# Forward substitution in the top half of a triangular solve, and level tiles of 64 columns, in the scan of an RWKV-7 layer on one NeuronCore

## The chip, the cores and the metric

The kernel runs on one core of a Trainium2 chip. The metric is the device time of one execution in microseconds (us); the time before is 1505.27 us, the median of three runs. Engines: TensorE (PE for its products, PEld for the loads of weights, which run beside the products), VectorE (DVE), ScalarE (ACT), GpSimd (POOL), SyncE (SP, which issues most transfers).

## What is computed

A decoder trunk of two blocks over 256 tokens of 1024 channels in float32: a pooling and gating mixer with a dense feed-forward block, then an RWKV-7 time mixing with 16 heads of 64 channels and a block of experts (two of eight per token). The change lies in the time mixing. Its core is a recurrence over the tokens with a 64 x 64 state per head:

```python
def step(S, inp):
    r_t, w_t, k_t, v_t, kk_t, a_t = inp
    sa = jnp.einsum('bhij,bhj->bhi', S, -kk_t)
    S = (S * w_t[:, :, None, :]
         + sa[..., None] * (kk_t * a_t)[:, :, None, :]
         + v_t[..., None] * k_t[:, :, None, :])
    y = jnp.einsum('bhij,bhj->bhi', S, r_t)
    return S, y
_, ys = lax.scan(step, S0, (tmajor(rh), tmajor(wh), tmajor(kh), tmajor(vh), tmajor(kk), tmajor(ah)))
```

## The kernel before

The kernel is written for each engine by hand: each engine's instructions stand in the order of its function, and semaphores tie the engines together. The time mixing takes its 256 tokens in two chunks (`c` = 0, 1) of 128. Within a chunk the recurrence is a triangular system per head: with a strictly lower triangular A (128 x 128), the kernel needs U = (I - A)^-1 R. R, the right side, is the product of a second causal matrix with the values and, in chunk 1, a product with the state `ST`. From U come the outputs and, in chunk 0, the state.

**The inverse.** `XT[c]` holds the transposed inverse, built bottom up. VectorE inverts the diagonal blocks of 16 tokens for all heads together, column by column (`recur`, 15 steps of two instructions, fed by TensorE's `block_rows`). `spread` puts them on the diagonal of `XT`. Then come the levels `v` = 0, 1, 2, which join blocks of 16 to 32, of 32 to 64 and of 64 to 128. A level is: `turned` (TensorE transposes `XT` by the identity, ScalarE copies its even blocks to `Xv`), `level_Y` (A times those), a masked copy to `Yv` on VectorE, `level_X` (Y times the odd blocks), and an add into the odd blocks of `XT` on VectorE. The third level is written as `top_Y` and `top_X`, with copies on ScalarE. After it `solved` multiplies the whole inverse (128 x 128) with the right side, and VectorE copies the result to `Us`.

**The order on TensorE.** The heads are handled in two groups of eight (`pair`). Levels of chunk 0 alternate with `block_rows(1, ...)`, which feed VectorE's `recur(1, ...)`. Levels of chunk 1 alternate with the group norm of chunk 0 (`gn_mean`, `head_sums`, `head_spread`). 22 transposes of the identity without use stand ahead of the first `turned(0, 0)`. There ScalarE also clears the two `Yv` tiles (semaphore `level_Y_zeroed`). On VectorE, `masked(0, gg)` makes parts of A causal, which the right side and the outputs need (semaphore `scan_A_causal`). After `outputs(1)` come the group norm, the output projection (`wo`), the router and the experts. The experts' weights come through SyncE's queue into the `ring` buffer; their first four loads wait for places in the scan (`level_X`, `U`, `Y`).

In the profile's shapes, 128*64 is a weight tile of 128 rows and 64 columns, and 64*64 one of 64 rows and 64 columns. A float32 product of the kernel stands there as two instructions with a load of weights each; a transpose stands as one.

Of the kernel before, what the change touches and what calls it, by code (L numbers as in the profile page):

```python
# [43 lines left out]
for _name, _w in (("ident", 128), ("ones", 128), ("upto", 128), ("before", 128), ("upto2", 128), ("heads", 128), ("iota", 128),  # L44
                  ("cum", 256), ("blk16", 128), ("mask4", 64), ("mask5", 64), ("eye16", 16), ("par", 2), ("hsel", 142),
                  ("invcnt", 4 * T)):
    CONST[_name] = (CW, CW + _w)
    CW += _w
# [7 lines left out]
def constants():  # L56
# [15 lines left out]
    put("blk16", s // 16 == t // 16)  # L72
    h4, h5 = np.arange(64)[None, :] // 16, np.arange(64)[None, :] // 32
    put("mask4", (s // 32 == h4) & (s % 32 >= 16))
    put("mask5", (s // 64 == h5) & (s % 64 >= 32))
# [31 lines left out]
def trunk(nc, I, cst_dram, cols_dram, out, stop=None):  # L107
    ctx = ExitStack()
    with ctx:
# [285 lines left out]
        def rows_product(pe, lhs, w, bank, done):  # L395
# [21 lines left out]
        l_tr, l_xe, l_y, l_yd, l_ya, l_xu, l_xd, l_x6 = (sem(x) for x in (  # L417
            "level_T", "level_T_copied", "level_Y", "level_Y_masked", "top_Y_copied", "level_X", "level_X_added",
            "top_X_copied"))
# [51 lines left out]
        XT = [ru(4 + c).rearrange("p (g l t) -> p g l t", g=4, l=4) for c in range(2)]  # L471
        Yv = [ru(6 + v).rearrange("p (g l t) -> p g l t", g=4, l=4) for v in range(2)]
        Xv = [wu(3, 1024, 1024 * v).rearrange("p (g l t) -> p g l t", g=4, l=4) for v in range(2)]
        Y6 = ru(13, 1024).rearrange("p (g n) -> p g n", g=4)
# [3 lines left out]
        Us = flatT[:, 0:1024].rearrange("p (g n) -> p g n", g=4)  # L478
# [35 lines left out]
        def lev(c, v, pair):  # L514

            return 6 * c + 2 * v + pair + 1

        def masked_at(c, v, pair):

            return 4 * c + 2 * v + pair + 1  # L520

        def turned_at(c, v, n):

            return 12 * c + 4 * v + n + 1

        TURN_BANK = (0, 1, 4, 5)
# [60 lines left out]
        def rwkv_pe(pe):  # L587
# [157 lines left out]
            def right_side(c, pair):  # L745
                pe.wait_ge(a_pm, 4 * c + 2 * pair + 2)
                pe.wait_ge(l_xe, turned_at(c, 2, pair))
                for gg, l, k, o, at in heads_of(pair):
                    dst = psum[:, pair, at:at + HD]
                    last = nc.tensor.matmul(dst, A_all[c][:, gg, l, 2, :], v_row[:, c * D + k * P + o:c * D + k * P + o + HD],  # L750
                                            start=True, stop=(c == 0))
                    if c == 1:
                        last = nc.tensor.matmul(dst, AR[:, k, c, 0, :], ST[:, k, o:o + HD], start=False, stop=True)
                last.then_inc(t_r, 1)

# [3 lines left out]
            pe.wait_ge(y_zero, 3)  # L759

            def turned(c, v):
                for gg in range(4):
                    if v == 0:
                        pe.wait_ge(x_full, 2 * c + gg // 2 + 1)
                        if c == 1 and gg == 2:
                            pe.wait_ge(t_sc, 2)
                    elif v == 2 and gg >= 2:
                        pe.wait_ge(l_xd, masked_at(c, 1, 1))
                    else:
                        pe.wait_ge(l_xd, masked_at(c, v - 1, gg // 2))  # L770
                    for l in range(4):
                        last = nc.tensor.transpose(psum[:, TURN_BANK[gg], l * P:(l + 1) * P], XT[c][:, gg, l, :], ident)
                    last.then_inc(l_tr, 1)

            def level_Y(c, v):
                for pair in range(2):
                    pe.wait_ge(l_xe, turned_at(c, v, 2 * pair + 1))
                    if v == 0 and c == 1:
                        pe.wait_ge(t_yc, pair + 1)
                    for gg, l, k, o, at in heads_of(pair):  # L780
                        for i in range(2):
                            hs, n = slice(HD * i, HD * i + HD), slice(32 * i, 32 * i + 32)
                            last = nc.tensor.matmul(psum[hs, 2 + pair, at + 32 * i:at + 32 * i + 32], A_all[c][hs, gg, l, 0, hs],
                                                    Xv[v][hs, gg, l, n], start=True, stop=True)
                    last.then_inc(l_y, 1)

            def level_X(c, v, pair):
                pe.wait_ge(l_yd, masked_at(c, v, pair))
                if pair == 0:
                    pe.wait_ge(l_xe, turned_at(c, v, 3))  # L790
                for gg, l, k, o, at in heads_of(pair):
                    odd = XT[c][:, gg, l, :].rearrange("p (b h t) -> p b h t", h=2, t=B0 << v)[:, :, 1, :]
                    for i in range(2):
                        hs, n = slice(HD * i, HD * i + HD), 2 >> v
                        last = nc.tensor.matmul(psum[hs, 4 + pair, at + 32 * i:at + 32 * i + 32], Yv[v][hs, gg, l, hs],
                                                odd[hs, n:2 * n, :] if i else odd[hs, 0:n, :], start=True, stop=True)
                last.then_inc(l_xu, 1)

            def top_Y(c):
                for pair in range(2):  # L800
                    pe.wait_ge(l_xe, turned_at(c, 2, 2 * pair + 1))
                    for gg, l, k, o, at in heads_of(pair):
                        last = nc.tensor.matmul(psum[HD:P, 2 + pair, at:at + HD], A_all[c][:, gg, l, 0, HD:P],
                                                Xv[0][:, gg, l, :], start=True, stop=True)
# [1668 lines left out]
```

## Time and profile before

| | |
|---|---|
| median of three runs | 1505.27 us (1505.21 to 1505.7) |
| the profiled execution | 1507.26 us, span 1505.4 us |
| granted TensorE clock, mean | 0.996 of full speed |
| busy share: PE, DVE, ACT, POOL | 98%, 83%, 67%, 1% |
| first turn of chunk 0's levels on TensorE | at 414.46 us |
| outputs of chunk 0, of chunk 1 on TensorE | at 445.16 us, at 486.66 us |
| first product of the experts | at 542.01 us |

The span is the time from the first to the last instruction of the profiled execution, which took 1.86 us more than it and 1.99 us more than the median of the runs. The scan's levels and their ends fill some 75 us of the 1505; the experts, from 542 us on, fill most of the rest. Times in the timeline view count from the span's start. A view can show an instruction up to 0.1 us earlier or later than the chain of work does, where instructions overlap.

### The profile page before, as it was taken

To read this page: it belongs to the slowest core of one execution; us is meant where nothing else is said; L and a number is where in the kernel's file an instruction comes from. 1 tells how busy PE (TensorE), PEld (TensorE's weight loads), DVE (VectorE), ACT (ScalarE), POOL (GpSimd) and SP (SyncE) were. 2 spreads that over 40 slices of the span, in tenths; PEclk is the share of its full clock that TensorE was granted. 3 is DMA by queue.
4 is the path that set the end of the run, shared out by engine and by line. 5 is a ranking of instruction groups with operands and counts; after the bars stand their busy time and mean duration, and the time that the engine had idled before them with its cause. 6 is when DMAs were issued, how large, how long until landed. Compare 5 with 4: busy or idle time off the path is not lost.

```text
span 1505.4 us, 22041 instructions
## 1 busy us (share of the span) xinstructions
PE 1474.2 (98%) x8088; PEld 1226.9 (82%) x8088; DVE 1242.6 (83%) x1375; ACT 1009.8 (67%) x1157; POOL 22.2 (1%) x19
## 2 busy tenths in 40 slices
PE   8999999999899999999999999999999999999997
PEld 5888888799798588888888888888888888888885
DVE  3756666787885289999999999999999999999997
ACT  2544444663523178888888888888888878888885
POOL 0000000000000020000000000000000000000200
PEclk9999999999999999999999999999999999999998
DMA  9889553036405499999999999999999999999990
GB/s 361 326 271 301 175 168 112 1 117 217 141 2 178 174 322 372 395 392 395 396 392 396 394 368 388 390 365 383 394 366 373 393 386 362 395 380 362 349 369 28
DMA packets 206696, 453.57 MB, mean 301 GB/s; under 512 B 8881, under 2 KB 46257, under 8 KB 206386
## 3 DMA queue, kind: packets, MB, share of 16 engines
q1 hardware_dynamic: 203154, 446.12, 80.6%
q0 software_dynamic: 1280, 4.20, 1.1%
q10 hardware_dynamic: 2208, 2.50, 0.5%
q8 instruction: 38, 0.62, 0.2%
q14 instruction: 16, 0.13, 0.0%
HBM read 437.58 MB, written 23.60 MB: 306 GB/s over the span
## 4 chain that ended last, share of the span: by engine, by line
PE 92%; DVE 5%; ACT 2%; DMA 1%; issue 0%; DVEq 0%; ACTq 0%
PE psum L1591 20%; PE psum L1593 20%; PE psum L1592 20%; PE psum L2401 5%; PE psum L2404 3%; PE psum L902 2%; PE psum L2325 2%; PE psum L2365 2%; PE psum L2366 2%; PE psum L2367 2%; PE psum L600 2%; PE psum L1609 2%; PE psum L2318 1%; PE psum L696 1%; DVE time_mix_parts L1150 1%; PE psum L722 1%
## 5 line engine op out<-in xcount | busy, mean ns | idle before, releaser
L1799 DVE TENSOR_TENSOR w_lo<-ring,w_hi 128x1024 fp32r<-128x1024 f32 x672 | 811.0, 1224 | 63.5 <-ACT w_hi L1693 15.8
L1693 ACT ACTIVATE w_hi<-ring 128x1024 fp32r<-128x1024 f32 x672 | 711.3, 1062 | 172.5 <-PE psum L1593 172.4
L1591 PE MATMUL psum<-w_hi,xg_split 128*128 128x512 f32 x896 | 353.5, 395 | 0.3 <-DVE xg_split L1890 0.3
L1593 PE MATMUL psum<-w_lo,xg_split 128*128 128x512 f32 x896 | 349.4, 390 | 0.0
L1592 PE MATMUL psum<-w_hi,xg_split 128*128 128x512 f32 x896 | 348.8, 389 | 0.0
L1593 PEld LDWEIGHTS psum<-w_lo,xg_split 128*128 128x128 f32 x896 | 168.1, 188 | 35.8
L1591 PEld LDWEIGHTS psum<-w_hi,xg_split 128*128 128x128 f32 x896 | 168.3, 188 | 34.1 <-DVE xg_split L1890 0.6
L1592 PEld LDWEIGHTS psum<-w_hi,xg_split 128*128 128x128 f32 x896 | 168.4, 188 | 33.6
L1591 PE MATMUL psum<-w_hi,ht_split 128*128 128x512 f32 x448 | 176.0, 393 | 0.0
L1593 PE MATMUL psum<-w_lo,ht_split 128*128 128x512 f32 x448 | 174.6, 390 | 0.0
L1592 PE MATMUL psum<-w_hi,ht_split 128*128 128x512 f32 x448 | 174.4, 389 | 0.0
L2235 DVE TENSOR_TENSOR f_lo<-ring,f_hi 128x1024 fp32r<-128x1024 f32 x66 | 79.5, 1223 | 51.3 <-ACT f_hi L2124 51.3
L2124 ACT ACTIVATE f_hi<-ring 128x1024 fp32r<-128x1024 f32 x66 | 69.0, 1056 | 52.4 <-PE psum L2404 30.6
L1591 PEld LDWEIGHTS psum<-w_hi,ht_split 128*128 128x128 f32 x448 | 84.1, 188 | 19.4 <-issue 2.3
L1593 PEld LDWEIGHTS psum<-w_lo,ht_split 128*128 128x128 f32 x448 | 84.1, 188 | 17.8
L1592 PEld LDWEIGHTS psum<-w_hi,ht_split 128*128 128x128 f32 x448 | 84.1, 188 | 17.1
L2401 PE MATMUL psum<-x_split,f_hi 128*128 128x512 f32 x352 | 88.9, 393 | 0.9 <-DVE x_split L360 0.4
L2401 PEld LDWEIGHTS psum<-x_split,f_hi 128*128 128x128 f32 x352 | 63.6, 189 | 14.2 <-DVE x_split L360 1.4
L600 PE MATMUL psum<-mixed_parts,time_mix_parts 128*128 128x256 f32 x448 | 64.6, 283 | 1.4 <-DVE time_mix_parts L1150 1.0
L600 PEld LDWEIGHTS psum<-mixed_parts,time_mix_parts 128*128 128x128 f32 x448 | 58.4, 192 | 1.7 <-DVE time_mix_parts L1150 1.2
L2404 PEld LDWEIGHTS psum<-x_split,f_lo 128*128 128x128 f32 x352 | 48.0, 190 | 3.4
L2404 PE MATMUL psum<-x_split,f_lo 128*128 128x256 f32 x352 | 49.1, 282 | 0.0
(370 smaller groups left out, 1488.7 us busy)
## 6 DMA issues: line engine op xcount, KB each, us to landing
ring<-o_moe_wg_dram SPq DMA_DIRECT2D x56, 2048.0 KB, 10.8
ring<-o_moe_wu_dram SPq DMA_DIRECT2D x56, 2048.0 KB, 11.3
ring<-o_moe_wd_dram SPq DMA_DIRECT2D x56, 2048.0 KB, 11.3
ring<-e_ffn_wg_dram SPq DMA_DIRECT2D x11, 1024.0 KB, 5.5
ring<-e_ffn_wu_dram SPq DMA_DIRECT2D x11, 1024.0 KB, 8.7
ring<-e_ffn_wd_dram SPq DMA_DIRECT2D x11, 1024.0 KB, 11.1
expert_rows<-work SPq DMA_DIRECT2D x1, 8192.0 KB, 27.9
ring<-e_w_in_dram SPq DMA_DIRECT2D x2, 2048.0 KB, 18.1
```

The costliest lines, as they stand in the source:

```text
L600: last = nc.tensor.matmul(psum[0:rows, n % 8, 0:width], l, r, start=(i == 0), stop=(i == len(lhs_rhs) - 1))
L902: return nc.tensor.matmul(psum[:, n, :], YT[:, k, (n // 2) * P:(n // 2 + 1) * P], wo_s[n % 2][:, k, :], start=(k == 0), stop=(k == KT - 1))
L1591: nc.tensor.matmul(dst, x_hi, hi, start=first, stop=False)
L1592: nc.tensor.matmul(dst, x_lo, hi, start=False, stop=False)
L1593: return nc.tensor.matmul(dst, x_hi, lo, start=False, stop=last_)
L1609: last = nc.tensor.transpose(psum[:, 6, f * P:(f + 1) * P], SIL[c % 2][:, f * P:(f + 1) * P], ident)
L1693: nc.scalar.activation(w_hi[:, (4 * i + n) % 4, :], piece(i, n), ACT.Copy).then_inc(m_hi, 1)
L1799: V.tensor_tensor(w_lo[:, r, :], piece(i, n), w_hi[:, r, :].bitcast(F32), ALU.subtract).then_inc(m_lo, 1)
L2124: nc.scalar.activation(as_piece(f_hi, i, what), ffn_piece(what, c, n), ACT.Copy).then_inc(f_phi, 1)
L2235: nc.vector.tensor_tensor(as_piece(f_lo, i, what), ffn_piece(what, c, n), as_piece(f_hi, i, what).bitcast(F32), ALU.subtract).then_inc(f_p ...
L2401: nc.tensor.matmul(psum[:, bank, :], hi[:, k, :], x_tile(k).rearrange("p h t -> p (h t)"), start=(k == 0), stop=False)
L2404: last = nc.tensor.matmul(psum[:, bank, T:2 * T], lo[:, k, :], x_tile(k)[:, 1, :], start=False, stop=(k == KT - 1))
```

## The change

The third level goes. In its place the system is solved in two halves of 64 tokens. `right_side` makes the top half of R, `solved` multiplies it with the top half's inverse (64 x 64), and the result `Us` is copied by ScalarE. Then `right_side` makes the low half, with one product more per head that subtracts A's lower left quarter times the top of `Us`, and `solved` multiplies it with the low half's inverse. `XT`, `Xv` and `Yv` keep only the diagonal quarters, so each tile is 64 columns wide. `turned` no longer transposes 128 x 128 tiles. It multiplies each 64 x 64 quarter with the even columns of the identity, so that only those blocks are made. The add in `level_X` becomes one instruction over 128 rows, the two clears and `spread` cover half the columns, and the four `masked(0, gg)` each move one place ahead on VectorE. GpSimd's clear of `Y6` goes.

```diff
             def turned(c, v):
-                for gg in range(4):
+                for pair in range(2):
...
-                    for l in range(4):
-                        last = nc.tensor.transpose(psum[:, TURN_BANK[gg], l * P:(l + 1) * P], XT[c][:, gg, l, :], ident)
+                    for gg, l, k, o, at in heads_of(pair):
+                        for hs in tops:
+                            even = ident[:, hs].rearrange("p (b h t) -> p b h t", h=2, t=B0 << v)[hs, :, 0, :]
+                            last = nc.tensor.matmul(psum[hs, pair, at // 2:at // 2 + 32], XT[c][hs, gg, l, :], even,
+                                                    start=True, stop=True)
                     last.then_inc(l_tr, 1)
...
+            top, low = slice(0, HD), slice(HD, P)
+
+            def solved(c, pair, rows):
+                if rows == top:
+                    pe.wait_ge(l_xd, lev(c, 1, pair))
+                    pe.wait_ge(t_rc, 4 * c + pair + 1)
+                else:
+                    pe.wait_ge(t_rc, 4 * c + 2 + pair + 1)
+                for gg, l, k, o, at in heads_of(pair):
+                    last = nc.tensor.matmul(psum[rows, 4 + pair, at:at + HD], XT[c][rows, gg, l, :],
+                                            Rs[rows, gg, HD * l:HD * l + HD], start=True, stop=True)
+                last.then_inc(t_u, 1)
+
+            def right_side(c, pair, rows):
+                pe.wait_ge(a_pm, 4 * c + 2 * pair + 2)
+                if rows == low:
+                    pe.wait_ge(t_uc, 4 * c + pair + 1)
+                upto = slice(0, rows.stop)
+                for gg, l, k, o, at in heads_of(pair):
+                    dst = psum[rows, pair, at:at + HD]
+                    vv = v_row[upto, c * D + k * P + o:c * D + k * P + o + HD]
+                    last = nc.tensor.matmul(dst, A_all[c][upto, gg, l, 2, rows], vv, start=True, stop=(c == 0 and rows == top))
+                    if c == 1:
+                        last = nc.tensor.matmul(dst, AR[:, k, c, 0, rows], ST[:, k, o:o + HD], start=False, stop=(rows == top))
+                    if rows == low:
+                        last = nc.tensor.matmul(dst, A_all[c][top, gg, l, 0, low], Us[top, gg, HD * l:HD * l + HD],
+                                                start=False, stop=True)
+                last.then_inc(t_r, 1)
...
-            turned(1, 2)
-            right_side(1, 0)
-            top_Y(1)
-            right_side(1, 1)
-            top_X(1)
-            solved(1)
+            for rows in (top, low):
+                for pair in range(2):
+                    right_side(1, pair, rows)
+                for pair in range(2):
+                    solved(1, pair, rows)
             outputs(1)
```

On TensorE, behind the second level of chunk 0 and its block products, the kernel before has the third turn (L772), the right side (L750), top Y (L803) and the next block products (L722). The shape in a row is that of the output.

```order
L772 MATMUL psum<-cst,ring 128x128 [waits level_X_added]
L772 MATMUL psum<-cst,ring 128x128 x3
L750 MATMUL psum<-work,ring 128x64 [waits level_T_copied,scan_A_causal]
L750 MATMUL psum<-work,ring 128x64 x7
L803 MATMUL psum<-work,ring 64x64 [waits level_T_copied,level_Y_zeroed]
L803 MATMUL psum<-work,ring 64x64 x7
L803 MATMUL psum<-work,ring 64x64 [waits level_T_copied]
L803 MATMUL psum<-work,ring 64x64 x7
L722 MATMUL psum<-work,xnT 128x64 [waits column_product]
```

At the same place the changed kernel has the right side's top half (its L799) around the block products (L713), and solved (L787) for both groups of heads.

```order
L799 MATMUL psum<-work,ring 64x64 [waits scan_A_causal]
L799 MATMUL psum<-work,ring 64x64 x7
L713 MATMUL psum<-work,xnT 128x128 [waits column_product]
L713 MATMUL psum<-work,xnT 128x112
L713 MATMUL psum<-work,xnT 128x96
L713 MATMUL psum<-work,xnT 128x80
L799 MATMUL psum<-work,ring 64x64 [waits scan_A_causal]
L799 MATMUL psum<-work,ring 64x64 x7
L787 MATMUL psum<-ring 64x64 [waits R_copied,level_X_added]
L787 MATMUL psum<-ring 64x64 x7
```

The turn of 128 x 128 tiles is gone, and solved comes ahead of the last block products, over 64 rows and columns.

Further on in chunk 1, the changed kernel's TensorE has this in the low half of the right side: the second matrix times the values (L799, weights of 128 rows), the state's product (L801, 128 rows) and A's quarter times the top of U (L803, 64 rows), head after head.

```order
L799 MATMUL psum<-work,ring 64x64 [waits U_copied,scan_A_causal]
L801 MATMUL psum<-work 64x64
L803 MATMUL psum<-ring 64x64
L799 MATMUL psum<-work,ring 64x64
L801 MATMUL psum<-work 64x64
L803 MATMUL psum<-ring 64x64
L799 MATMUL psum<-work,ring 64x64
L801 MATMUL psum<-work 64x64
```

Before, the right side of chunk 1 was one row of products whose weights were all 128 rows by 128 columns. Now weights of 128 and of 64 rows follow one another within each head.

## Rows read from the trace of the kernel before

**Rows 1.** The page: busy time of each engine, share of the span, instructions.

```profile
PE 1474.2 (98%) x8088; PEld 1226.9 (82%) x8088; DVE 1242.6 (83%) x1375; ACT 1009.8 (67%) x1157; POOL 22.2 (1%) x19
```

**Rows 2.** Waits after 530 us: who for whom, us in total, times, longest.

```profile
ACT w_hi L1693 <- PE psum L1593: 172.4, 572, 2.5
```

**Rows 3.** Stretches: busy time (instructions) by engine, PE clock, DMA share, GB/s.

```profile
400.00:500.00 100.00, 95.14 (x1282) 83.68 (x1281) 64.32 (x144) 34.63 (x63) 0.94 (x1) 1.00 0.31 109
...
532.00:533.00 1.00, 1.00 (x6) 1.00 (x5) 0.93 (x6) 1.00 (x2) 0.00 (x0) 0.50 1.05 430
...
640.00:740.00 100.00, 100.00 (x457) 82.72 (x456) 93.05 (x86) 81.98 (x88) 0.00 (x0) 1.00 1.04 394
```

**Rows 4.** Timeline from 410 us: start, length, instruction, [idle before <- what ended it].

```profile
410.70 3.71 ACT L1094 ACTIVATE ring<-cst 128x2048 f32<-128x2048 f32 x2
410.86 2.38 PEld L758 LDWEIGHTS psum<-cst 128*128 128x128 f32 x22 [1.52 <-ACT ring L1044]
...
414.46 1.97 PE L772 MATMUL psum<-cst,ring 128*128 128x128 f32 x16 [0.98 <-ACT ring L1094]
```

**Rows 5.** Timeline, turns of the levels that waited, chunk 0 and 1.

```profile
423.88 1.09 PE L772 MATMUL psum<-cst,ring 128*128 128x128 f32 x8 [0.64 <-DVE ring L1319]
...
454.40 1.06 PE L772 MATMUL psum<-cst,ring 128*128 128x128 f32 x8 [0.44 <-DVE work L1380]
...
461.91 1.98 PE L772 MATMUL psum<-cst,ring 128*128 128x128 f32 x16 [0.83 <-DVE ring L1319]
```

**Rows 6.** Chain of work, chunk 0: start, us to the next piece, what.

```profile
416.43 1.99 PE psum L783 x64
...
431.01 1.93 PE psum L772 x16
...
434.67 2.01 PE psum L803 x32
...
441.51 3.71 PE psum L822 x32
445.23 0.38 PE psum L835 x4
```

**Rows 7.** Timeline of TensorE: third turn, outputs of chunk 1, experts' first product.

```profile
469.50 2.26 PE L772 MATMUL psum<-cst,ring 128*128 128x128 f32 x16
...
486.66 0.19 PEld L834 LDWEIGHTS psum<-work 128*64 128x64 f32 x2
...
542.01 0.50 PE L1591 MATMUL psum<-w_hi,xg_split 128*128 128x512 f32 x1 [0.32 <-DVE xg_split L1890]
```

**Rows 8.** Timeline, loads of weights of L803 and of what follows.

```profile
434.60 1.94 PEld L803 LDWEIGHTS psum<-work,ring 128*64 128x64 f32 x32
...
436.61 0.97 PEld L722 LDWEIGHTS psum<-work,xnT 128*128 128x128 f32 x8
```

**Rows 9.** Timeline where the weights' shape changes without a semaphore.

```profile
446.74 0.44 PE L836 MATMUL psum<-ring,work 128*64 128x128 f32 x4
...
447.10 0.30 PEld L842 LDWEIGHTS psum<-xnT,xn 128*128 128x128 f32 x2 [0.17 <-issue]
...
297.08 3.72 PE L633 MATMUL psum<-ring,work 128*128 128x256 f32 x16
...
300.73 0.74 PEld L636 LDWEIGHTS psum<-ring,work 32*128 32x128 f32 x16 [0.33 <-issue]
```

**Rows 10.** Stretches of 0.01 us, L803 alone: products (in flight), loads, clock, DMA.

```profile
434.70:434.71 0.01, 0.01 (x1) 0.01 (x2) 1.00 0.00 0
434.71:434.72 0.01, 0.01 (x2) 0.01 (x3) 1.00 0.00 0
```

**Rows 11.** Groups from 410.8 to 494 us: busy us, mean ns, idle before.

```profile
L803 PE MATMUL psum<-work,ring 128*64 128x64 f32 x64 | 4.2, 224 | 0.0
...
L1061 ACT ACTIVATE ring<-psum 64x512 f32<-64x512 f32 x4 | 2.4, 592 | 1.6 <-PE psum L803 1.6
...
L1319 DVE TENSOR_TENSOR ring<-ring,psum 64x256 f32<-64x256 f32 x16 | 6.6, 416 | 0.3
```

More of the change, by code:

```diff
@@ L780, in level_Y @@
                     for gg, l, k, o, at in heads_of(pair):
[L781 to L784, printed above, removed]
+                        for hs in tops:
+                            last = nc.tensor.matmul(psum[hs, 2 + pair, at // 2:at // 2 + 32], A_all[c][hs, gg, l, 0, hs],
+                                                    Xv[v][hs, gg, l, :], start=True, stop=True)
@@ L817, in solved @@
-            def solved(c):
-                for pair in range(2):
-                    pe.wait_ge(t_rc, 2 * c + pair + 1)
-                    pe.wait_ge(l_x6, 2 * c + pair + 1)
-                    for gg, l, k, o, at in heads_of(pair):
-                        last = nc.tensor.matmul(psum[:, (6, 0)[c] + pair, at:at + HD], XT[c][:, gg, l, :],
-                                                Rs[:, gg, HD * l:HD * l + HD], start=True, stop=True)
-                    last.then_inc(t_u, 1)
+            top, low = slice(0, HD), slice(HD, P)
@@ L858, in rwkv_pe @@
             level_X(0, 1, 1)
+            right_side(0, 0, top)
             block_rows(1, 3)
[L860 to L863 removed]
+            right_side(0, 1, top)
+            solved(0, 0, top)
+            solved(0, 1, top)
             block_rows(1, 4)
[L865 to L868 removed]
+            for pair in range(2):
+                right_side(0, pair, low)
+            for pair in range(2):
+                solved(0, pair, low)
             outputs(0)
@@ L1097, in rwkv_act @@
             turned(0, 1)
-            turned(0, 2)
-            right_side(0, 0)
-            top_Y(0)
-            right_side(0, 1)
-            top_X(0)
+            for half in range(2):
+                for pair in range(2):
+                    right_side(0, pair, half)
+                for pair in range(2):
+                    solved(0, pair, half)
             outputs(0)
@@ L1112, in rwkv_act @@
             last.then_inc(gw_done, 1)
-            turned(1, 2)
-            right_side(1, 0)
-            top_Y(1)
-            right_side(1, 1)
-            top_X(1)
+            for half in range(2):
+                for pair in range(2):
+                    right_side(1, pair, half)
+                for pair in range(2):
+                    solved(1, pair, half)
             outputs(1)
@@ L1373, in rwkv_dve @@
             spread(1)
-            solved(0)
             masked(1, 0)
```

172 lines of the change are left out of this document (57 added, 115 removed).

## The prediction

> **What bounds the kernel now.** The page comes first: TensorE is busy 98% of the span, the other engines less [rows 1]. Then the waits after 530 us, the experts: ScalarE waits for TensorE 172.4 us in all [rows 2], and in a stretch of 100 us there TensorE is busy all 100 at full clock while the DMA share is 1.04 [rows 3]. So the weights arrive in time, TensorE sets the pace, and a later or earlier start of the experts moves the end by as much. The same holds between the scan's last product and the experts: everything there hangs on events that move with the scan. What the change is worth is read between 410 and 487 us, on TensorE. In this stretch its clock is 1.00 throughout [rows 3], it has few waits [rows 4, 5], and both sweeps through the top level are one unbroken chain of TensorE groups [rows 6]. VectorE and ScalarE matter only where a row names them in brackets.
>
> **The prices.** A product in float32 stands as two instructions, each with its weight load. Three steady rates are in the trace. Weights 64 columns wide, all products in the same column half: 32 instructions take 2.01 us, 0.06 each [rows 6, 8]. Weights 64 wide with the two diagonal quarters in turn: 64 instructions in 1.99 us, 0.03 each [rows 6]. Weights 128 wide: 32 in 3.71 us, 0.116 each [rows 6].
>
> The fourth price is that of a change of shape (rows times columns of the weights, as 128*64). Where the shape stays, the loader has no gap: the 32 loads of L803 cover 1.94 us although a semaphore stands in the middle [rows 8]. Where it changes, the loader stands still. From 128*64 to 128*128, with no semaphore between, it idles 0.17 us [rows 9]. From 128*128 to 32*128, again with no semaphore, where only the rows change, it idles 0.33 us behind products of 256 columns [rows 9]. I read this as: the loads of the new shape start only when the last product of the old one is through. For the new case (weights 64 wide, 64 columns streamed) I take the end of L803: its last product starts at 436.68 - 0.22 = 436.46 [rows 6, 11], the next shape's load at 436.61 [rows 8], so 0.15 us. After a change the first load is not hidden either: L803's second product starts 0.11 us after its first (434.71 against 434.60) [rows 8, 10]. A product that stands alone between two changes thus costs 0.11 + 0.15 = 0.26 to 0.27 us, where in an unmixed row it costs 0.12. A change costs 0.145 us.
>
> The Trainium skill has a rule that speaks against this change. Its page "TensorEngine Tiling (Array Packing)", in "Key Properties", says "Changing tiling mode (not just tile) drains the TensorE", and it lists 128x64 and 64x64 as modes of their own. By that rule the sum is the one with every change paid; read as if a change were free, it would be the first rival below. The idle loads of [rows 9] agree with the rule, but no row has 128*64 beside 64*64.
>
> **The change, part by part.**
> - *Start of the levels, -1.2 us.* The two clears of Y shrink from 2048 to 1024 columns, so from 3.71 us in all to some 2.0, and end at 412.7 instead of 414.4. TensorE's 22 idle transposes end at 413.24, and the first turn begins there instead of at 414.46 [rows 4]. The spreading on VectorE, half as long now, is ahead of that.
> - *Turning, 0.* Before, 16 transposes take 1.9 us (1.93 in the chain) [rows 6]. Now 32 products in diagonal quarters, 64 instructions at 0.03, take 1.99. ScalarE's copies are halved in number, off the path.
> - *Levels of chunk 0, -0.7 us.* Each second add was two instructions of 0.42 us [rows 11]; now it is one over 128 rows. The second half of the second turn waited 0.64 us for it [rows 5]; that goes. Three of the four masks of A that move ahead of level work fall into VectorE's idle time before its level operations; where one makes a level operation late (0.4 us at most by my count of the order), a group of block products on TensorE covers it.
> - *Levels of chunk 1, -0.7 us.* Two waits are there, 0.44 and 0.83 us [rows 5]. The first goes, since the turn no longer writes the banks in which the state lies. Of the second about 0.5 us stays, being a chain on VectorE (mask of Y, centring, add): I count 0.7 of the 1.27.
> - *Top of chunk 0, +1.3 us.* Before: third turn to outputs, 445.23 - 431.01 = 14.2 [rows 6], less 1.0 for the block products that stay between them [rows 8]: 13.2. Now: right side top, 16 products of one shape, 2.0; solved top 2.0; solved low 2.0; right side low has per head one product of 128*64 and one of 64*64, so 32 products and 32 changes at 0.265: 8.5. Together 14.5.
> - *Top of chunk 1, +5.7 us.* Before: 486.66 - 469.50 = 17.2 [rows 7]. Now the right side also has the state's product, of shape 128*64. Top: 64*64 and 128*64 in turn, 32 products with 32 changes, 8.5. Low: 128*64, 128*64, 64*64, per head 3 x 0.12 + 2 x 0.145 = 0.65, times 16 is 10.4. Solved twice 2.0. Together 22.9.
> - *Copies on ScalarE.* Right side to solved and solved to right side now go through ScalarE four times a chunk instead of twice. One copy of a 64-row tile is 0.59 us [rows 11] and some 0.2 of latency; the other pair's group of at least 1.0 us stands in between each time, so it costs 0. Were that cover gone it would be 0.8 us for each of 8 hand-overs.
> - *The rest, 0.* The clear on GpSimd went out of the way before 411 us; the expert loads hang on the same events, and the one that waits for the solved values starts at chunk 1's outputs, while its first use is behind 542.0 [rows 7].
>
> Sum: -1.2 - 0.7 + 1.3 - 0.7 + 5.7 = +4.4 us. The profiled execution took 1507.26 us with a span of 1505.4; against that, 1511.7 and 1509.8. The runs' median is 1505.27, which gives **1509.7**.
>
> **Bounds.** The 96 changes hold 96 x 0.145 = 13.9 us of it. From below, a change costs nothing: +4.4 - 13.9 = -9.5. From above, the 0.33 us of idle loader is paid each time: 96 x 0.33 = 31.7, or +22; but that row has products four times as wide, so it is an outer end only. I take 0.145, from the row nearest in size. The sign turns at 9.5 / 96 = 0.10 us a change.
>
> **The rivals.**
> - *A change of rows alone is free within a column half (faster).* Both shapes use the same 64 columns, and only the inner half of the array's rows is switched. Then the top of chunk 0 is 9.9 us and that of chunk 1 13.8, the chain is one of products at 0.12, and the time 1495.8. For it: no row shows this very pair. Against it: the row from 128*128 to 32*128, where the columns stay. Chance 0.14.
> - *Half is paid.* Only one direction drains, or the load overlaps the drain: 96 x 0.07, so -9.5 + 6.9 = -2.6, 1502.7. The idle of some changes in the trace is shorter than of others (0.17, 0.33), which leaves room. Chance 0.12.
> - *The clock falls.* In the mixed stretches the array does in 0.265 us what it does in 0.12 in an unmixed row, so it works less densely than in any group of [rows 6]. The trace has one fall, to 0.50 at 532 us [rows 3], behind transposes and products of 8 columns. If one of the three mixed stretches (8.5, 8.5, 10.4 us) ran half its length at 1.2 GHz, it would add 4 to 5 us: 1514, and up to 1518 for one whole. Against: level groups with short waits between never lost it. Chance 0.14.
> - *All 96 changes paid, as summed.* Chance 0.60, own range 1507 to 1512.
>
> **How the numbers follow.** The range leaves out the free case and the far end of the clock case, and goes from 1500.5 to 1514.5. A difference of 0.2% (3.0 us) is what a measurement of this kernel can tell. Faster than 1502.3: the free case and 0.05 of the half case, 0.19. Slower than 1508.3: the clock case's 0.14 and 0.45 out of the likeliest's 0.60, together 0.59 (the other 0.15, with changes nearer 0.13 us, stays within 0.2%). Between: that 0.15 and 0.07 of the half case, 0.22.
>
> **What would show it.** In the profile after: pairs of products in the right side's low part at 0.26 to 0.27 us against 0.12 in solved, with loader idle between them; the first turn at 413.3; no wait above 0.1 us between the pairs; the experts' first product 4 to 5 us later than at 542.0 [rows 7]. The prediction is wrong if the right side runs at 0.12 a product (then 1496), or if hand-overs through ScalarE show as waits of TensorE.

## The result

| | us |
|---|---|
| kernel before, median of 4 runs | 1505.41 (1505.21 to 1505.7) |
| changed kernel, median of 4 runs | 1534.13 (1532.66 to 1535.08) |
| ratio, 95% interval | 1.019 (1.0172 to 1.0207) |
| predicted | 1509.7 (1500.5 to 1514.5) |

Slower, as forecast, but by 28.7 us instead of 4.4. The page of the changed kernel, busy time and instructions of TensorE and the granted clock in 40 slices:

```profile
span 1532.7 us, 22516 instructions
PE 1502.7 (98%) x8344; PEld 1247.1 (81%) x8344; DVE 1231.5 (80%) x1359; ACT 1003.8 (65%) x1145; POOL 20.8 (1%) x18
...
PEclk9999999999976799999999999999999999999998
```

TensorE is as busy as in [rows 1], 98%; the new thing is the dip of the clock in three slices. Stretches of TensorE place it:

```profile
435.00:440.00 5.00, 5.00 (x30) 0.59 0.00 0
...
450.00:455.00 5.00, 5.00 (x46) 0.70 0.02 3
455.00:460.00 5.00, 5.00 (x96) 1.00 0.43 131
...
470.00:475.00 5.00, 3.89 (x86) 0.84 0.03 6
475.00:480.00 5.00, 5.00 (x52) 0.50 0.28 75
480.00:500.00 20.00, 20.00 (x121) 0.50 0.23 87
500.00:515.00 15.00, 15.00 (x108) 0.50 0.06 8
515.00:520.00 5.00, 5.00 (x71) 0.72 1.02 390
```

In each line stand the stretch, its length, TensorE's busy time and instructions in it, the granted clock, the DMA share and GB/s. The clock is at 0.50, which is 1.2 GHz, for about 17 us in chunk 0 and 44 us in chunk 1; before it was 1.00 from 400 to 500 us [rows 3]. The share of busy time does not show it: 5.00 of 5.00 at either level. The chain of work in chunk 0 (start, us, what):

```profile
413.53 1.99 PE psum L752 x64
...
427.82 0.95 PE psum L799 x16
...
433.78 0.26 PE psum L799 x2
434.04 0.26 PE psum L803 x2
434.29 0.26 PE psum L799 x2
...
435.83 0.32 PE psum L799 x2
436.15 0.40 PE psum L803 x2
```

The first turn and the right side's top half stand where they were forecast, at 413.5 (before 414.46 [rows 4]) and 427.8. The mixed row (L799 with weights 128*64, L803 with 64*64) runs at 0.257 us a product, and after 2.1 us of it the clock falls: each product then takes 0.40. Now the timeline of chunk 1:

```profile
469.04 1.93 PE L763 MATMUL psum<-work,ring 64*64 64x32 f32 x58
472.07 0.36 PE L763 MATMUL psum<-work,ring 64*64 64x32 f32 x5 [1.11 <-issue]
...
473.35 2.03 PE L544 MATMUL psum<-work,cst 64*128 64x128 f32 x16
...
477.04 0.45 PE L799 MATMUL psum<-work,ring 64*64 64x64 f32 x2
...
513.05 0.69 PE L815 MATMUL psum<-work 128*64 128x128 f32 x2
...
569.56 0.50 PE L1553 MATMUL psum<-w_hi,xg_split 128*128 128x512 f32 x1 [0.32 <-DVE xg_split L1852]
```

Two things were not in the forecast. In the middle of a level group TensorE stands still for 1.11 us with no semaphore ("issue"), and the clock falls at 473.4 us, ahead of the mixed rows, which then run wholly at 0.50 (477.0 to 513.0).

Where the time went, place by place against [rows 4, 7] and the table of before: outputs of chunk 0 at 448.56 instead of 445.16, +3.4 (forecast -0.6); from there to the top of chunk 1 28.5 us instead of 24.3, +4.1 (forecast -0.7); the top of chunk 1 36.0 instead of 17.2, +18.9 (forecast +5.7); from its outputs to the experts' first product 56.5 instead of 55.4, +1.2 (forecast 0). Together +27.6, and the spans differ by 27.3.

One thing behind the scan matters for every comparison of medians below. In some executions the clock falls once more at the router, ahead of the experts, and in others it doesn't. First the changed kernel, in which it stays, then the same kernel with a later load (an experiment below), in which it falls:

```profile
560.00:565.00 5.00, 4.75 (x42) 1.00 1.03 408
```

```profile
555.00:560.00 5.00, 5.00 (x26) 0.50 1.04 388
```

From the group norm's product behind the outputs of chunk 1 to the experts' first product the one takes 47.8 us and the other 50.4; the kernel before took 48.9. So two medians can differ by up to 2.7 us through the router alone, and the scan is better compared by itself. Here "the scan" is the time from the start of the 22 idle transposes to that product of the group norm, in the profiled execution: 82.2 us before, 110.9 us in the changed kernel.

### The profile page after: what moved, and what is told of

The parts are those of the page before. It is cut to its first block, busy times and chain, and to the rows that moved or that the text cites. A ratio compares the mean times of both kernels' runs of the same rounds, so it can differ in the third digit from the quotient of the medians.

```text
span 1532.7 us, 22516 instructions
## 1 busy us (share of the span) xinstructions
PE 1502.7 (98%) x8344; PEld 1247.1 (81%) x8344; DVE 1231.5 (80%) x1359; ACT 1003.8 (65%) x1145; POOL 20.8 (1%) x18
## 4 chain that ended last, share of the span: by engine, by line
PE 92%; DVE 5%; ACT 1%; DMA 1%; issue 1%; DVEq 0%; ACTq 0%
PE psum L1553 20%; PE psum L1555 20%; PE psum L1554 20%; PE psum L2363 5%; PE psum L2366 3%; PE psum L881 2%; PE psum L2287 2%; PE psum L2327 2%; PE psum L2328 2%; PE psum L2329 2%; PE psum L591 2%; PE psum L1571 2%; PE psum L799 1%; PE psum L2280 1%; PE psum L687 1%; PE psum L803 1%
## 5 line engine op out<-in xcount | busy, mean ns | idle before, releaser
L1761 DVE TENSOR_TENSOR w_lo<-ring,w_hi 128x1024 fp32r<-128x1024 f32 x672 | 810.8, 1224 | 63.2 <-ACT w_hi L1655 15.6
## 6 DMA issues: line engine op xcount, KB each, us to landing
ring<-o_moe_wg_dram SPq DMA_DIRECT2D x56, 2048.0 KB, 10.5
```

The source lines that it names most:

```text
L1761: V.tensor_tensor(w_lo[:, r, :], piece(i, n), w_hi[:, r, :].bitcast(F32), ALU.subtract).then_inc(m_lo, 1)
```

## The experiments

Two theories to begin with (theories A and C of the expectations; theory B is that weights of 64*64 let the clock fall by themselves). **Mixing:** the rows in which products with 128*64 and 64*64 weights follow one another cost their changes of shape and pull the clock down. **Levels:** the level and turning products of 32 columns, with their waits, let the clock fall by themselves. Run beside the experiments, the kernel before had medians of 1505.25 to 1505.84 us, with single runs up to 1511.64.

**Sorting the right side.** Within each group of eight heads first all products of one matrix, then the next; 96 changes of shape become 12. The first product of a group alone starts the accumulation in its bank.

```diff
-                    last = nc.tensor.matmul(dst, A_all[c][upto, gg, l, 2, rows], vv, start=True, stop=(c == 0 and rows == top))
-                    if c == 1:
-                        last = nc.tensor.matmul(dst, AR[:, k, c, 0, rows], ST[:, k, o:o + HD], ...)
+                    last = nc.tensor.matmul(dst, A_all[c][upto, gg, l, 2, rows], vv, start=(at == 0), ...)
+                if c == 1:
+                    for gg, l, k, o, at in heads_of(pair):
...
+                        last = nc.tensor.matmul(dst, AR[:, k, c, 0, rows], ST[:, k, o:o + HD], start=False, ...)
...
```

> The changed kernel, only that the right side's products are sorted by the shape of their weights within each group of eight heads: first the second matrix times the values, then the state's products, then those with the top of U. The same products and the same sum; changes of shape within the right side fall from 96 to about 10. Theory A (a change of shape costs 0.14 us at full clock, and the stretches that mix shapes are what lets the clock fall): pairs at 0.12 us a product, clock at 1.00 through both tops, time 1496 to 1499 us. Theory B (weights of 64*64 as such let the clock fall): the clock falls at about the same places and the time stays above 1515 us. Theory C (the second fall, which in the changed kernel's trace begins at 473 us, before the mixed stretch of chunk 1, belongs to the levels): the first fall goes, the second stays, 1500 to 1512 us.

Measured 1502.4 us (1497.03 to 1507.13, 10 runs; ratio 0.9978, 0.9957 to 0.9998). The chain of chunk 0's low right side in it:

```profile
433.94 1.07 PE psum L799 x16
435.01 1.07 PE psum L809 x16
436.08 1.08 PE psum L799 x16
```

The same 16 instructions that took 2.06 us mixed take 1.07, and in the profiled execution (1500.61 us) the clock is 1.00 through the scan, although chunk 1's level group stops for 0.83 us there too. So the order of these products alone is worth 31.7 us, more than the whole loss. The spread follows the clock: the fastest run had a mean of 0.999, the slowest 0.989; where the clock fell in the slow ones no profile shows.

**One shape throughout.** As before, and the top half's product takes all 128 rows of A and of the values (the extra rows are zeros of the causal mask), so that chunk 1's top half changes shape nowhere.

```diff
-                upto = slice(0, rows.stop)
+                upto = slice(0, P)
```

> As e1_sorted, and the right side's first product takes all 128 rows for the top half too (the rows added hold zeros of the causal matrix, so the result is the same). In chunk 1 the top then has no change of shape at all. Theory A: the same as e1_sorted within 1 us, since a row of 128*64 and one of 64*64 both run at 0.12 us a product. Theory B: faster than e1_sorted by several us, since fewer products are 64*64. Theory C: as e1_sorted.

Measured 1501.87 us (1500.26 to 1504.22; 0.9958 to 0.9984): 0.5 us less than the sorted kernel, within its spread. Its trace has a stop of 0.81 us without a semaphore in the level group of chunk 1, and the clock at 0.64 and 0.68 in the two stretches of 5 us behind it.

**Turning by products alone.** The kernel before, with its first two turns done by 64*64 products with even identity columns; the third level is as before. ScalarE's copies of these turns are two instead of four, and the wait for the copied state moves from the turn to `level_X`.

```diff
+                if v < 2:
+                    for pair in range(2):
...
+                            for i in range(2):
+                                hs = slice(HD * i, HD * i + HD)
+                                last = nc.tensor.matmul(psum[hs, pair, at // 2:at // 2 + 32], XT[c][hs, gg, l, hs], even, ...)
```

> The kernel before, where only the first two levels turn by products of 64*64 quarters with even identity columns; the third level stays, with its transposes. 64 instructions in place of 16 in each of four turns. Theory A: no mixed stretch, clock 1.00, the same time as before within 1 us. Theory C (the levels themselves let TensorE run out of instructions for 1.1 us near 471 us and the clock fall near 473 us): a gap marked issue and a clock below 1.00 between 465 and 490 us, time 1508 to 1520 us.

Measured 1520.34 us (1517.72 to 1521.9; ratio 1.0095, 1.0068 to 1.0123). Stretches of it around the second turn of chunk 0:

```profile
422.00:424.00 2.00, 1.52 (x46) 1.00 0.02 4
424.00:426.00 2.00, 1.77 (x61) 1.00 0.03 8
426.00:428.00 2.00, 2.00 (x43) 0.61 0.00 0
428.00:434.00 6.00, 6.00 (x74) 0.50 0.01 3
```

No mixed row, and still +15 us: behind waits for VectorE (TensorE busy 1.52 and 1.77 of 2.00) and short products the clock falls, and once more in 465 to 470 us (0.74), where TensorE waits 0.83 us for VectorE and then stops for 1.12 us without a semaphore. The second theory is right too, in a kernel with such waits. The changed kernel's levels have fewer waits, and its clock fell there only behind the stop.

**Pairs of shapes by themselves.** The kernel before, with nine groups of 16 products ahead of the levels, each behind 8 products of 512 columns. The cut shows the third group.

```diff
+            for _ in range(8):
+                nc.tensor.matmul(psum[0:64, 2, 0:64], ident[0:128, 0:64], ident[0:128, 0:64], start=True, stop=True)
+                nc.tensor.matmul(psum[0:64, 2, 0:64], ident[0:64, 0:64], ident[0:64, 0:64], start=True, stop=True)
```

> The kernel before; in place of the 22 idle transposes ahead of the levels stand nine groups of 16 idle products of 64 columns each, each behind 8 dense products of 512 columns that keep the clock up: one shape 128*64; one shape 64*64; those two in turn; two 64*64 tiles of different rows in turn; the two column halves of 128*64 in turn; the diagonal 64*64 quarters in turn; 128*128 with 128*64; 128*128 with 64*128; 64*128 with 64*64. The time itself says nothing, the product rates are read from the trace. Theory A: 0.12 us a product in one shape, 0.06 in two column halves, 0.26 for every pair of different shapes, whichever of rows or columns differs, and 0.12 or less for two tiles of one shape. If only changes of rows cost, 128*128 with 128*64 stays at 0.17 (the mean of its two steady rates).

Chain of work, the mixed group:

```profile
439.58 0.26 PE psum L768 x2
439.84 0.25 PE psum L769 x2
440.10 0.26 PE psum L768 x2
```

Alone, 16 products of 128*64 take 2.01 us, and so do 16 of 64*64; in turn they take 4.1, 0.257 each. Two 64*64 tiles in other rows, two column halves of 128*64 and the diagonal quarters in turn take 1.0 to 1.1 us for 16: a change of place costs nothing, a change of shape 0.257 - 0.12 = 0.13 to 0.14 us. It makes no difference whether rows or columns change: 128*128 with 128*64 takes 0.625 us a pair, and 128*128 with 64*128 0.73, where the unmixed rates (0.232 for weights 128 wide [rows 6], 0.12 for 64) give 0.35 and 0.46; both leave 0.27 for two changes. The Trainium skill's "TensorEngine Tiling (Array Packing)", "Key Properties", says the same, that changing the mode, not just the tile, drains TensorE; it has no price. In or right behind each of the four groups of mixed shapes the clock fell, and nowhere else among the nine.

**Long rows of one kind.** Again the kernel before, with rows of 10 to 23 us ahead of the levels, each behind 24 products of 512 columns. The cut shows the second row.

```diff
+            for _ in range(192):
+                nc.tensor.matmul(psum[0:64, 2, 0:32], ident[0:64, 0:64], ident[0:64, 0:32], start=True, stop=True)
+                nc.tensor.matmul(psum[64:128, 2, 0:32], ident[64:128, 64:128], ident[64:128, 0:32], start=True, stop=True)
```

> The kernel before, with five added rows of small products on TensorE ahead of the levels, each behind 24 products of 512 columns: (1) 96 products 64*64 of 64 columns in one quarter; (2) 192 products 64*64 of 32 columns in each of the two diagonal quarters in turn, as the level tiles have them; (3) 96 transposes of 128*128; (4) 24 pairs of 128*64 and 64*64; (5) 96 products 128*64 in one column half. None of them waits for anything. The question is behind which of them the granted clock falls. Mixed shapes are the cause: only behind (4), some 2 us after its start, as in the kernel after; (1), (2), (3) and (5) stay at 1.00. Small tiles are the cause: also (2), in the second half of its 12 us at 0.03 us an instruction, and perhaps (1). A row that keeps 1.00 takes 0.12 us a product ((1), (5): 11.5 us), 0.06 us a pair of diagonal products ((2): 23 us or half of it), 0.12 us a transpose (11.5 us); at half clock each takes up to twice that.

Stretches of TensorE, in order: 64*64; diagonal 64*64 of 32 columns; transposes; the mixed row, twice; 128*64.

```profile
431.00:442.00 11.00, 11.00 (x190) 1.00 0.01 1
463.00:485.00 22.00, 22.00 (x751) 1.00 0.01 4
506.00:517.00 11.00, 11.00 (x99) 1.00 0.01 1
537.00:541.00 4.00, 4.00 (x30) 1.00 0.02 4
541.00:555.00 14.00, 14.00 (x71) 0.51 0.00 0
577.00:589.00 12.00, 12.00 (x194) 1.00 0.01 3
```

This separates the theories cleanly: without waits, small tiles keep 1.00 for 22 us, and the mixed row alone loses it, 3.6 us after its start. The Trainium skill's "TensorE: Matmul & The Clock Gate", "Part 4: PE-mode transpose", says that the full clock doesn't engage for transposes; here 96 of them in a row, in float32, ran 10.5 us at 1.00. So a clock that is up stays up through them, against that sentence; whether it would rise during transposes no run here shows.

**The stop: a later load.** On the one-shape kernel, the transfer of the output projection's weights (4 MB) waits for one more event, the first half of chunk 1's last level.

```diff
             sp.wait_ge(t_y, 2)
+            sp.wait_ge(l_xu, lev(1, 1, 0))
             w = I["o_wo"].rearrange("a (k p) n -> p (a k) n", p=P)
```

> The kernel of the one-shape experiment (right side sorted, all rows in its top half), with one more wait on the queue that loads the weights of the output projection, so that this load starts behind the first half of chunk 1's last level instead of ahead of it. If the stop of 0.8 us inside the last level's products (no semaphore, and the 4 MB load under way) is the load in the way of the instructions of TensorE, it goes, and the clock does not fall at 460 us: 1499 to 1500 us, 2 us less than the one-shape experiment's 1501.9. If the stop has nothing to do with the load, it stays at 0.8 us and the time at 1500 to 1504.

Measured **1496.44 us** (1494.95 to 1497.07; ratio 0.9934, 0.9913 to 0.9955), 5.4 us less than the one-shape kernel, the fastest of all. Of the 5.4 us, the scan of the profiled executions has 4.1 (72.9 us instead of 77.0), and the router's fall is in the one-shape kernel's profile and not in this one. The level group in its timeline, and 40 us of its scan:

```profile
457.69 2.06 PE L764 MATMUL psum<-work,ring 64*64 64x32 f32 x64
```

```profile
440.00:480.00 40.00, 39.82 (x791) 1.00 0.47 163
```

64 instructions in one piece, no stop, and the clock stays at 1.00 although the load, and those of the experts behind it, now run beside the right side and what follows (DMA share 1.04 to 1.08 from 465 to 495 us).

**Wider turning products.** On the one-shape kernel, 64 columns of the identity instead of the 32 even ones; ScalarE picks the even blocks. Then both edits together.

```diff
-                            last = nc.tensor.matmul(psum[hs, pair, at // 2:at // 2 + 32], XT[c][hs, gg, l, :], even, ...)
+                            last = nc.tensor.matmul(psum[hs, pair, at:at + HD], XT[c][hs, gg, l, :], ident[hs, hs], ...)
```

> The kernel of the one-shape experiment, with the turning products 64 columns wide (the whole identity quarter) and the even blocks picked by ScalarE's copy, as before; all level products keep their 32 columns. If the short turning products are what lets the clock fall around the levels, it stays at 1.00 there and the median is at 1499 to 1500 us, the spread of the runs gone (the one-shape experiment had 1500.3 to 1504.2). If turning costs by its columns, the four turns take 4 x 2 us more (1510 us). If neither, 1501 to 1503 us, and the fall at 460 to 470 us stays.

> The later load and the wide turning products together, on the one-shape experiment. If each takes away a cause of the falling clock, the clock has only the fall at the router, and the time is 1498.5 to 1499.5 us, the shortest so far. If one of them has no effect, it equals the other one's time within 0.5 us.

Measured 1500.56 us (1497.84 to 1501.94) and 1496.74 (1496.18 to 1499.22). The wide turn costs nothing (a turn takes 2.08 us instead of 2.05 to 2.06) but doesn't save the clock: behind a stop of 0.96 us it is 0.70 and 0.62 in two stretches. With the load moved, width makes no difference. Here the clock goes with the stop, not with the columns; the sorted kernel's profile, with a stop of 0.83 us and no fall, says that a stop doesn't bring the fall every time.

**The later load on the changed kernel, and on the kernel before.** The same added wait.

> The changed kernel with one edit: the queue's load of the output projection's weights (4 MB) waits for the first half of chunk 1's last level as well. The stretches of mixed shapes stay. If the load stands in the way of TensorE's instructions, the stop of 1.11 us inside the last level goes, and the clock, which now falls at 473.4 us and stays at 0.50 until 517.6, falls only some 2 us inside the mixed stretch of chunk 1. Then it is 1.1 us for the stop, and about 3.5 us of work between 473.4 and the mixed stretch's third microsecond done at full speed: 1528 to 1530 us instead of 1534.1. If the mixed shapes alone are the cause of everything, 1533 to 1535; if the fall at 473.4 is what holds the clock down for the whole stretch of 44 us, 1510 to 1516.

> The kernel before with the same later load of the output projection's weights. Its trace has no stop without a semaphore in the levels, and the clock is at 1.00 throughout the scan. So if the load's only harm is that stop, nothing is won: 1505 to 1506 us, and the gain of the late load in the sorted kernels belongs to the changed levels with their short products. If the load slows the scan in other ways, 1499 to 1502.

Measured 1529.83 us (1528.57 to 1531.61; 1.0133 to 1.0181), and 1506.7 (1504.77 to 1510.82) beside 1505.84 without it, ratio 1.0003 (0.9988 to 1.0018). In the first the stop is gone, the clock is at 1.00 until 478.7 us, 5.4 us into chunk 1's mixed row, and falls there all the same. By the medians 4.3 us of the 28.7 are the stop's, with what the clock lost behind it; the scan alone is 7.0 us shorter (103.9 instead of 110.9), and in this kernel's profile the fall at the router takes 2.7 of them back. The kernel before gains nothing. Its profile holds a surprise, in the timeline and the stretches:

```profile
461.24 3.56 PE L773 MATMUL psum<-cst,ring 128*128 128x128 f32 x16 [0.83 <-DVE ring L1320]
```

```profile
460.00:461.00 1.00, 0.41 (x14) 1.00 0.00 0
461.00:462.00 1.00, 0.76 (x4) 0.57 0.00 0
```

Behind the same wait as in [rows 5], 0.83 us, the clock fell, which it had not in the profiled execution of before. So that place is near the edge in the kernel before too. That its slower runs (up to 1511.64 us, at a mean clock of 0.994) are executions in which the clock fell there is likely, not shown.

**Filling the waits.** The kernel with turning products, the later load, and 6 idle transposes ahead of each second half of the second turn.

```diff
+                            if pair == 1:
+                                for _ in range(6):
+                                    nc.tensor.transpose(psum[:, 2, 0:P], ident, ident)
                             pe.wait_ge(l_xd, masked_at(c, 0, pair))
```

> The kernel before with only the two first turns of a chunk done by 64*64 products (1520.3 us before, with the clock falling at 426 and 466 us), and two more edits: the late load, and 6 idle transposes of 128*128 in each of the two waits of 0.6 to 0.8 us in front of the second turn's second half. If a wait followed by short products is what lets the clock fall, the clock stays at 1.00 and the time is at the kernel before: 1504.5 to 1507 us. If the short turning products do it by themselves, the fall at 426 us stays and the time is 1512 to 1518.

Measured 1515.11 us (1512.71 to 1515.79), 5.2 less than without the load's wait and the fill; the stop is gone with the later load, as in the other kernels. Timeline of chunk 1's second turn:

```profile
461.52 1.12 PE L777 MATMUL psum<-cst,ring 64*64 64x32 f32 x32 [0.83 <-DVE ring L1339]
462.57 1.39 PE L771 MATMUL psum<-cst 128*128 128x128 f32 x6
```

In chunk 0, where the fill covers the wait, the clock stays at 1.00 from 425 to 460 us. In chunk 1 the wait stands ahead of the first half, where the fill is not, and the clock falls at the first transposes behind it (0.78 in 460 to 465 us, then 0.50). Both of the expected outcomes, one in each chunk. Chunk 0, which the later load doesn't touch, shows that what lets the clock fall in the levels is the wait with short products around it. The fill ahead of chunk 1's first half wasn't tried.

**How much mixing.** The fastest kernel, with chunk 0's low right side alone (32 products) sorted not in eights but mixed fully, in twos and in fours. The cut shows twos.

```diff
+                    for g in range(0, 8, 2):
+                        for gg, l, k, o, at in hh[g:g + 2]:
+                            nc.tensor.matmul(..., A_all[c][upto, gg, l, 2, rows], vv, start=(at == 0), stop=False)
+                        for gg, l, k, o, at in hh[g:g + 2]:
+                            last = nc.tensor.matmul(..., A_all[c][top, gg, l, 0, low], Us[top, ...], ...)
```

> The fastest kernel so far (sorted right side, late load: 1496.4 us) with chunk 0's low right side alone back in mixed order, 128*64 and 64*64 in turn, 32 products. By the trace of the changed kernel a mixed product costs 0.257 us at full clock instead of 0.12, 32 x 0.14 = 4.5 us; by the same trace the clock falls some 2.2 us after the mix begins, and stays at 0.50 for about 17 us: the rest of the mix at 0.404 instead of 0.257 is 3.4 us more, and solved and outputs at half clock some 5 us more. So with the clock 1508 to 1511 us; were it the shapes alone, 1501 us.

> The kernel with chunk 0's low right side mixed (1508.1 us; sorted in eights 1496.4), its 32 products now sorted in groups of two heads: two of 128*64, two of 64*64, and so on, 16 changes of shape in place of 32. If the granted clock follows how often the shape changes in the stretch, it stays at 1.00 and only 16 x 0.14 = 2.2 us are paid: 1498 to 1500 us. If any alternation within some microseconds lets it fall, the clock goes in the same place, 435 to 450 us, and the time is 1504 to 1508.

> The same with groups of four heads, 8 changes of shape in the stretch. If changes cost 0.14 us each and no clock: 1497 to 1498.5 us. If the clock falls here too, 1501 to 1506.

| changes of shape | us | more than in eights | the scan in the profile |
|---|---|---|---|
| 32, every product | 1508.08 (1506.04 to 1510.68) | 11.6 | 83.7, +10.7 |
| 16, in twos | 1499.0 (1496.86 to 1500.08) | 2.6 | 74.6, +1.7 |
| 8, in fours | 1498.32 (1495.75 to 1499.09) | 1.9 | 73.5, +0.6 |
| 4, in eights | 1496.44 (1494.95 to 1497.07) | 0 | 72.9 |

Stretches of the fully mixed kernel, then the chain and a stretch of the one in twos:

```profile
434.00:435.00 1.00, 1.00 (x9) 1.00 0.00 0
435.00:436.00 1.00, 1.00 (x8) 0.78 0.00 0
436.00:437.00 1.00, 1.00 (x7) 0.50 0.00 0
```

```profile
434.07 0.38 PE psum L802 x4
434.45 0.37 PE psum L805 x4
```

```profile
434.00:440.00 6.00, 6.00 (x71) 1.00 0.01 3
```

In twos, two products take 0.375 us, 0.13 more than unmixed: the price of one change. In twos there are 12 changes more than in eights, 12 x 0.135 = 1.6 us, and in fours 4 more, 0.5 us; that is the whole difference of the scans, and the clock takes nothing. The rest of the differences of medians is within the spread of the runs and the fall at the router, which the profiles in twos and in fours have and the one in eights has not. Fully mixed, 28 x 0.137 = 3.8 us are the changes, and the other 7 to 8 us the clock. The price is not in proportion to the changes: half of them cost less than a quarter.

## Why the prediction was wrong, step by step

The account of the runs: everything but mixing and the stop is worth 1496.4 - 1505.4 = -9.0 us; mixing costs 1529.8 - 1496.4 = 33.4 (up to 0.5 of it the rows of the top half); the stop and its clock 1534.1 - 1529.8 = 4.3. The scans of the profiles split it as 72.9 - 82.2 = -9.3, 103.9 - 72.9 = 31.0 and 110.9 - 103.9 = 7.0, without what the router does in single executions. Of the 31 for mixing, the 84 changes that the fastest kernel lacks are 84 x 0.137 = 11.5, and some 20 are the clock.

- *Start of the levels, -1.2:* borne out but for 0.2. The first turn is at 413.5 instead of 414.46 [rows 4]; the kernels' profiles begin this stretch up to 1.5 us apart, but from the start of the idle transposes it comes after 2.55 us instead of 3.60.
- *Turning, 0; levels of chunk 0, -0.7:* borne out in time. The turns take 1.93 to 1.99 us, and the right side comes at 427.8, 2.1 us ahead of where the next block products began before; forecast were 1.9. What was missed is the other property of these products, four times as many instructions as transposes.
- *Levels of chunk 1, -0.7:* wrong by 4.8 us in the changed kernel: part is outputs at half clock, part the stop and the half clock behind it. In the fastest kernel the levels from the first turn (447.20) to the right side (462.82) take 15.6 us, against 16.6 before and 15.9 forecast.
- *Top of chunk 0 and of chunk 1, products:* the rates were right, 0.257 against 0.265 mixed and 0.12 unmixed. With all changes free the forecast had 9.9 and 13.8 us (its own prices give 13.6 for the second); in the fastest kernel they take 10.3 (427.02 to 439.34 less 2.0 for block products) and 13.9 (462.82 to 476.69).
- *96 changes, 13.9 us:* right in mechanism and size, 96 x 0.137 = 13.2. That one price came from loads of weights that stood idle between other shapes [rows 8, 9]; the rivals "a change of rows is free" and "half is paid" fall.
- *Copies on ScalarE, 0:* borne out. The chain runs from TensorE to TensorE through both tops.
- **The failed step is that the sum puts the clock at nothing and leaves it to the rival "the clock falls".** The rival was seen, with a ground that the runs fit (the array does less in a mixed row than in any other), and given 0.14 and 4 to 9 us. The clock fell in every profile with such rows, and cost some 20. Two things were wrong in its working. The likelihood: "against: level groups with short waits between never lost it" set other products as evidence for a row that had none, and they do keep it for 22 us where nothing stops them (with waits between them they can lose it, as the turning products show). And the size: it was taken as half of one mixed stretch, while the clock stays down behind the row, in solved, outputs and the state's products (17 us in chunk 0), and in chunk 1 nearly from one end of the top to the other (36.0 us for 22.9).
- *Not in the forecast:* the stop of 1.11 us. It is in the profiles of all four kernels with changed levels and the 4 MB load at its old place (0.81 to 1.11 us) and of the one with turning products (1.12), in none of those with the load moved, and in no level group of the kernel before, which has a quarter of the instructions in its turns. The load isn't under way in the stop itself:

```profile
471.00:472.00 1.00, 0.00 (x0) 1.00 0.00 0
```

But a transfer of the queue that the profile calls "instruction" comes late behind it: 2.8 us after the start of chunk 1's second turn in each of those four (469.3 against 466.48 in the changed kernel), and 0.9 to 1.0 us after it in the six kernels with changed levels and the load moved. That the stop is TensorE waiting for its own instructions fits this; whose instructions the transfer brings the profile doesn't say, so the cause is argued, not shown.

The sum without any price for the changes was 1495.8 us. The one-shape kernel with the late load has 1496.4: the change does bring its 9 us where the order keeps shapes together and the load out of the way.

## What to carry to other kernels

Sort small products by the shape of their weight tiles, not by head: a change of shape costs 0.14 us here, and a row that changes with every product also lets the clock fall to half for itself and for what follows. Where a row changes shape with every product, count the half clock as the likely case, for the row and for some microseconds behind it, although TensorE shows 100% busy, and read the granted clock of stretches in the result first. Look at it also where the change did nothing: here a fall at the router moves single executions by up to 2.7 us. When a change multiplies an engine's instructions, look at which large transfers run beside them.

## What the runs showed of the hardware

- The clock fell 2.1 us into the mixed row of the changed kernel, 3.6 us into the added one, and with the later load 1.3 us (chunk 0) and 5.4 us (chunk 1) into the same rows; TensorE was 100% busy each time. It did not fall in 22 us of 32-column products, 10.5 us of transposes or 6 us of a row with a change after every second product.
- A change of weight shape costs 0.13 to 0.14 us, whether rows or columns change; a change of place within one shape costs nothing (16 products in 1.0 to 1.1 us).
- At half clock solved takes 3.60 us for 32 instructions against 2.00, 1.8 times; a mixed product takes 0.40 against 0.257, 1.6 times.
- In the sorted kernels several heads accumulate in one bank with their products interleaved, and only the first product over those partitions starts the accumulation.
